# Moving ten rows of an adaLN modulation pair from VectorE to GpSimd in a two-layer trunk on one Trainium2 core

## What is computed

```python
cond = jax.nn.silu(c)                                  # 2048
for l in range(DEPTH):
    mod = (cond @ w_ada[l] + b_ada[l])[:, None, :]     # 2048 x 12288 per layer
    sh1, sc1, g1, sh2, sc2, g2 = jnp.split(mod, 6, axis=-1)
    u = x * (1.0 + sc1) + sh1
    y = mixer(u)
    x = layer_norm(ALPHA * x + (1.0 + g1) * y, ln_g[l, 0], ln_b[l, 0])
    u = x * (1.0 + sc2) + sh2
    y = conv_ffn(u, w_up[l], conv_w[l], conv_b[l], w_down[l])
    x = layer_norm(ALPHA * x + (1.0 + g2) * y, ln_g[l, 1], ln_b[l, 1])
```

## Time and profile before

| | us |
|---|---|
| median of 3 runs | 2282.24 (2281.42 to 2286.51) |
| the profiled execution | 2279.88 |
| its span, first to last instruction | 2278.1 |
| TensorE busy in it | 2234.2 |
| VectorE busy | 1695.1 |
| ScalarE busy | 1009.2 |
| GpSimd busy | 8.3 |
| mean granted TensorE clock | 0.993 of full speed |

### The profile page before, as it was taken

One profiled execution on the slowest core, in us unless ns is written; L12 is line 12 of the kernel. 1 busy time (PEld: TensorE's weight loads), 2 busy tenths in 40 slices (PEclk: granted clock), 3 DMA queues, 4 the chain that ended last, 5 costly groups with the idle time before them and its releaser, 6 DMA issues. The chain is left out here.

```text
span 2278.1 us, 27917 instructions
## 1 busy us (share of the span) xinstructions
PE 2234.2 (98%) x11205; PEld 1855.7 (81%) x11205; DVE 1695.1 (74%) x1671; ACT 1009.2 (44%) x1011; POOL 8.3 (0%) x19
## 2 busy tenths in 40 slices
PE   7999999999999999999999999999999999999999
PEld 3777777888887888888788888878888888888886
DVE  2889999768878878788877767684688756565565
ACT  2445344454433444443355444434544334444432
POOL 1000000000000000000000000000000000000000
PEclk9999999999999999999999999999999999999999
DMA  9999899868889978889787777865688756565653
GB/s 375 388 409 350 296 329 349 283 214 277 286 282 342 309 271 290 268 278 330 289 311 255 278 255 251 305 212 167 204 279 283 264 189 204 192 193 186 223 190 105
DMA packets 392227, 612.66 MB, mean 269 GB/s; under 512 B 21113, under 2 KB 205073, under 8 KB 390562
## 3 DMA queue, kind: packets, MB, share of 16 engines
q1 hardware_dynamic: 387314, 608.29, 76.4%
q10 hardware_dynamic: 4336, 2.33, 0.3%
q0 software_dynamic: 448, 0.25, 0.0%
HBM read 608.70 MB, written 2.10 MB: 268 GB/s over the span
## 5 line engine op out<-in xcount | busy, mean ns | idle before, releaser
L939 DVE TENSOR_TENSOR w_lo<-w_raw,w_hi 128x2048 fp32r<-128x2048 f32 x380 | 847.7, 2233 | 387.3 <-ACT w_hi L598 336.2
L598 ACT ACTIVATE w_hi<-w_raw 128x2048 fp32r<-128x2048 f32 x380 | 710.2, 1870 | 831.1 <-PE banks L1443 496.9
L1575 PE MATMUL banks<-u_hl,w_hi 128*128 128x512 f32 x2368 | 575.6, 392 | 3.3 <-ACT hid_tok L638 1.8
L1575 PEld LDWEIGHTS banks<-u_hl,w_hi 128*128 128x128 f32 x2368 | 432.9, 188 | 90.4 <-ACT hid_tok L638 2.7
L1443 PE MATMUL banks<-w_hi,u_hl 128*128 128x512 f32 x1920 | 478.7, 402 | 10.8 <-ACT u_hl L663 3.8
L1443 PEld LDWEIGHTS banks<-w_hi,u_hl 128*128 128x128 f32 x1920 | 362.5, 192 | 95.3 <-issue 16.3
L1583 PEld LDWEIGHTS banks<-u_hl,w_lo 128*128 128x128 f32 x2368 | 308.4, 191 | 15.6 <-DVE w_lo L939 1.2
L1583 PE MATMUL banks<-u_hl,w_lo 128*128 128x256 f32 x2368 | 313.3, 283 | 0.3 <-DVE w_lo L939 0.3
L1443 PE MATMUL banks<-w_hi,hid_hi 128*128 128x512 f32 x688 | 270.1, 393 | 0.0
L1443 PE MATMUL banks<-w_hi,hid_lo 128*128 128x512 f32 x688 | 267.8, 389 | 0.0
L955 DVE SCALAR_TENSOR_TENSOR ada_acc<-ada_w,silu_c,ada_acc 128x1024 f32<-128x1024 f32 x187 | 239.3, 1280 | 17.7 <-DMA ada_w<-in_w_ada 11.6
(11 more groups left out here) (229 smaller groups left out, 1247.8 us busy)
## 6 DMA issues: line engine op xcount, KB each, us to landing
ada_w<-in_w_ada SPq DMA_DIRECT2D x352, 512.0 KB, 6.7
w_raw<-in_w_up SPq DMA_DIRECT2D x344, 512.0 KB, 4.7
w_raw<-in_w_down SPq DMA_DIRECT2D x152, 512.0 KB, 4.9
w_raw<-in_w_qkv SPq DMA_DIRECT2D x96, 512.0 KB, 4.7
w_raw<-in_w_in_ab SPq DMA_DIRECT2D x64, 512.0 KB, 9.2
ada_w_more<-in_w_ada SPq DMA_DIRECT2D x32, 512.0 KB, 10.8
w_raw<-in_w_out_ab SPq DMA_DIRECT2D x32, 512.0 KB, 6.3
w_raw<-in_w_o SPq DMA_DIRECT2D x32, 512.0 KB, 5.1
```

The costliest lines, as they stand in the source:

```text
L598: nc.scalar.activation(whi[:, u % HL_SLOTS, 0:width], raw[:, u % RAW_SLOTS, 0:width], ACT.Copy).then_inc(w_hi, 1)
L939: nc.vector.tensor_tensor(wlo[:, u % HL_SLOTS, 0:width], raw[:, u % RAW_SLOTS, 0:width], whi[:, u % HL_SLOTS, 0:width].bitcast(f32), ALU.s ...
L1575: ins = nc.tensor.matmul(bank[banks[s] + i][:, :], tile(whi, k, s, i), uhl[:, kt].rearrange("p a s -> p (a s)"), start=first and k == 0, s ...
```

## The change

GpSimd takes rows 0 to 9 of pair 8. For each it waits until the row has landed, multiplies it in place in its slot by its column of silu(c) (for row 0, into the accumulator), waits for that product, and adds it to the accumulator. The semaphore `a_on_pool` counts the rows that it has taken; SP waits for it before it loads another row into such a slot. The loads of these ten rows stand with units 40 to 44, two each; before, nine stood with units 40 to 45 and row 9 with unit 52. VectorE takes the last six rows, two in each of units 52 to 54, and waits for all ten of GpSimd's ahead of the first. `STEP_NO` numbers the rows without GpSimd's for the waits on `a_step`.

```diff
+POOL_PAIR, POOL_ROWS = 8, 10
...
-    put([(8, r) for r in range(9)], first - 8, [2, 1, 2, 1, 2, 1])
+    for n in range(POOL_ROWS):
+        loads.setdefault(first - 8 + n // 2, []).append((POOL_PAIR, n))
     loads[first - 2] = [(9, r) for r in range(PE_ROWS[9])]
     put([(9, r) for r in range(PE_ROWS[9], 7)], first, [3], 1)
     put([(9, r) for r in range(7, KT)], first + 1, [3, 3, 3])
-    put([(8, r) for r in range(9, KT)], first + 4, [3, 2, 2])
+    put([(8, r) for r in range(POOL_ROWS, KT)], first + 4, [2, 2, 2])
...
+    steps = sorted((row for row in order if row[0] != POOL_PAIR or row[1] >= POOL_ROWS), key=order.get)
+    steps = {row: i for i, row in enumerate(steps)}
...
                     of, k = ROW_OF[old]
-                    if k < PE_ROWS.get(of, 0):
+                    if of == POOL_PAIR and k < POOL_ROWS:
+                        sp.wait_ge(a_on_pool, k + 1)
+                    elif k < PE_ROWS.get(of, 0):
                         sp.wait_ge(a_on_pe, PE_BASE[of] + k + 1)
                     else:
-                        sp.wait_ge(a_step, A0 + old + 1)
+                        sp.wait_ge(a_step, A0 + STEP_NO[of, k] + 1)
...
-                    dve.wait_ge(a_step, A0 + ROW_NO[m, r - 1] + 1)
+                    if (m, r) == (POOL_PAIR, POOL_ROWS):
+                        dve.wait_ge(a_on_pool, POOL_ROWS)
+                    else:
+                        dve.wait_ge(a_step, A0 + STEP_NO[m, r - 1] + 1)
...
+            acc = acc_of(POOL_PAIR)
+            pool.wait_ge(sem("silu_c"), 1)
+            pool.wait_ge(a_sum, SUM_NO[6, 0] + 1)
+            for r in range(POOL_ROWS):
+                slot, loads = ada_slot(POOL_PAIR, r)
+                w = ada_row_at(slot)
+                to = w if r else acc[:, :]
+                pool.wait_ge(a_loaded[slot], 16 * loads)
+                ins = nc.gpsimd.tensor_scalar(to, w, silu_c[:, r:r + 1], None, ALU.mult)
+                if r:
+                    ins.then_inc(sem("pool_product"), 1)
+                    pool.wait_ge(sem("pool_product"), r)
+                    pool.wait_ge(a_on_pool, r)
+                    ins = nc.gpsimd.tensor_tensor(acc[:, :], w, acc[:, :], ALU.add)
+                ins.then_inc(a_on_pool, 1)
```

More of the change, by code:

```diff
@@ L204, in ada_plan @@
     assert taken == sorted(taken)
-    return at, loads, order, sums, number, folds
+    steps = sorted((row for row in order if row[0] != POOL_PAIR or row[1] >= POOL_ROWS), key=order.get)
+    steps = {row: i for i, row in enumerate(steps)}
+    return at, loads, order, steps, sums, number, folds
 def build(nc, A, out):
@@ L344, in build @@
         a_on_pe = sem("ada_on_pe")
+        a_on_pool = sem("ada_on_pool")
         a_sum = sem("ada_summed")
@@ L398, in build @@
               (1, "down_b"): 20}
-        ADA_ROWS, ADA_LOADS, ROW_NO, ADA_SUMS, SUM_NO, ADA_FOLDS = ada_plan()
+        ADA_ROWS, ADA_LOADS, ROW_NO, STEP_NO, ADA_SUMS, SUM_NO, ADA_FOLDS = ada_plan()
         ROW_OF = {i: row for row, i in ROW_NO.items()}
@@ L1497, in ada_sum @@
                     warm(WARM_SUMS[m])
-                pe.wait_ge(a_step, A0 + ROW_NO[m, KT - 1] + 1)
+                pe.wait_ge(a_step, A0 + STEP_NO[m, KT - 1] + 1)
                 pe.wait_ge(a_out, SUM_NO[m, k] + 1)
@@ L1647, in up_first @@
                         if not layer:
-                            pe.wait_ge(a_step, A0 + ROW_NO[9, PE_ROWS[9]] + 1)
+                            pe.wait_ge(a_step, A0 + STEP_NO[9, PE_ROWS[9]] + 1)
                     unit(u, [(k, 4 * j + k) for k in range(4)], (uhi, ulo), j == 0, j == 3,
```

## The result

| | before | after |
|---|---|---|
| median | 2283.47 (4 runs, 2281.42 to 2286.51) | 2308.97 (4 runs, 2306.07 to 2311.73) |
| the profiled execution | 2279.88 | 2309.84 |
| its span | 2278.1 | 2307.7 |
| mean granted clock | 0.993 | 0.987 |

The change makes the kernel slower by 25.5 us; the ratio of the times is 1.0116, with a 95% interval of 1.0104 to 1.0128. Forecast were 10 us more, in a range that ended at 2306. The sign and the place were right, the size was not.

A forecast was written before the change was run, and what follows sets the result against it. TensorE, 98% busy, was taken as the bound, time changing only at its waits and slow clock. Late norm +8.2, slow clock +3.4, vanished wait -1.6: +10.0, forecast 2292 us, range 2278 to 2306.

The forecast's parts named there:

- turn-taking: Rival, 22%: GpSimd advances only while VectorE runs nothing with two SBUF inputs; norm's transposes +19.4, in all some +18, about 2300.
- Where it would happen: Ahead of the MLP's norm: GpSimd's last row delays load (9, 3), its matmuls, warm-up and the transposes, +8.2 us.
- Break-even, 3.6 us a row: Row 9 done at 344.9 + 8p against the slot's old freeing at 373.7; each 0.1 us above delays the norm 0.8.
- One product and one row fit ahead of row 2: GpSimd's start: rows 0 and 1 are finished before row 2 lands at 344.9, so eight rows follow from there.
- I take the upper end, p = 4.7: GpSimd's time per row, from its memset's 0.95 per stream times five streams; row 9 then done at 382.5.
- ten more: Within the turn-taking rival: p = 4.7 in place of the middle 3.35 adds ten us to its some +18.
- The landing, 6.5 us: Ahead of the norm: row (9, 3), issued at 382.6 once GpSimd frees the slot, lands at 389.1.
- The slow clock: At the norm: TensorE, waiting long, probably falls to its lower clock, at the price seen at pair 9's sum, +3.4 us.
- The wait of 1.6 goes: At pair 9's sum: its last rows gain time behind a late norm, so TensorE's wait vanishes, -1.6 us.
- The removal on VectorE, at nothing: Before 373.7 us: taking nine row instructions off VectorE gains nothing, since TensorE's own work hides them.
- The 1.1 us on VectorE's chain: Ahead of the norm: VectorE's tail starts 1.1 us earlier; only 0.58 usable unless pair 9's rows come earlier too.
- The rival without change: Rival, 25%: p between 3.2 and 3.9, row 9 done between 370.5 and 376.1, time 2281.6 to 2284.

## Why the prediction was right in sign and wrong in size

Two terms failed: p, the time of a GpSimd row (4.7 taken, 5.36 measured alone), and turn-taking, which was a rival and not a term (10.1 us). By the prediction's own sum p = 5.36 alone would give +15.2 and 2297.4, inside the range; it is the turns that carry the time beyond 2306. Point by point, in the time of before:

- **Where it would happen: right.** GpSimd's last row, the load of (9, 3), its matmuls, the warm-up and the transposes end last, in that order, and TensorE's waits name the DMA.
- **Break-even, 3.6 us a row: right.** Products alone end at 374.0 and cost nothing; with six, eight and ten rows GpSimd ends 8.1, 15.4 and 26.2 past the point, and the norm's transposes are 6.2, 13.3 and 24.2 late.
- **"One product and one row fit ahead of row 2": wrong**, by 3.4. They last until 348.3, not 344.9 (351.93 - 3.6). GpSimd starts at 338.6 and needs 3.0 + 5.36 for them alone, already 347.0.
- **"I take the upper end, p = 4.7": this step failed.** A row alone takes 5.36. The bound was made by scaling the memset (0.95) by streams, which gave the product two streams and 1.9 us; it takes 2.84. The memset is an instruction of GpSimd with no arithmetic and no operand to read, and was no upper bound for one that has both. From 338.6 on, 3.0 + 9 x 5.36 = 51.2 puts the last row at 389.8, **+16.1** over 373.7.
- **Turn-taking as a rival, not a term: this failed as well.** It adds **10.1** to that (399.9 against 389.8). I had laid 22 us of VectorE's work on top of the middle p. Both ends of that sum were off, p too low and the turns too many, and +18 was still short. The "ten more" that it gives for p = 4.7, some +28, was the nearest to what happened, by an overcount of the turns. My evidence against it, the memset beside a split, was none, since it reads nothing.
- **The landing, 6.5 us: too long.** With the queues empty (share 0.28) row (9, 3) landed 3.9 us after its issue, **-2.6**.
- **The slow clock: right that it falls, its price too high here.** The granted clock is 0.50, but TensorE has almost nothing to do in it: the last row's matmuls and the warm-up take 3.2 instead of 1.9, **+1.3**; no full unit is hit (unit 48's first part takes 3.91). Of 16.1 + 10.1 - 2.6 + 1.3 the 0.6 of waiting that TensorE had before is to be taken off: 24.3, with 24.2 in the trace for the transposes and 25.5 in the medians.
- **"The wait of 1.6 goes": wrong.** It is 2.07. Pair 9's later rows stood in the same queue behind GpSimd, so they came as much later as the norm.
- **The removal on VectorE, at nothing: right,** and for a stronger reason than I gave: with nobody taking the rows the kernel gains nothing that can be measured. The 1.1 us on VectorE's chain went the other way: the prediction named that the weights of the next units are queued behind SP's wait, and put no price on it. ScalarE waited 6.44 for them and the split ahead of the norm started at 374.5 instead of 373.7; with the longer split and addition the norm's scaling starts 4.9 later than before.
- **The rival without change** rested on p under 3.9; a row takes 5.36 alone. The Trainium skill's word of one-input work at roughly line-rate (GPSIMD Engine Reference, section 4.1) stood on its side: the prediction's estimate from it, 1024 elements at 1.2 GHz, is 0.85 for the product, which takes 2.84 here, so the measurement decides against it. The Trainium skill's figure for the add (the same page, section 3.1) holds nearly: half of 4497 ns is an estimate of 2.25, and the sum takes 2.34 here.

No version of the idea tried here beats the kernel before. Of those that do all the work the nearest is the one with ScalarE's products, 2.7 us over; the two that are even with the kernel before leave work out.

## What to carry to other kernels

Before work is moved from a busy engine to an idle one, ask what the kernel would gain if that work vanished. Here it was nothing, at most 2.3 us, so every cost on the other side was a loss. GpSimd's price for an instruction is to be measured alone and beside what runs next to it, as VectorE's instructions lengthen it and are lengthened by it, small one-input ones included. And a slot that a slow engine frees late holds up the whole load queue behind it, the weights of other engines among them (ScalarE waited 6.44 us here).

## What was not expected of the hardware

- GpSimd's f32 product by a column (one input) takes 2.84 us for 128x1024, longer than its sum of two tensors, 2.34; VectorE's takes 0.75. At 512 columns it is 1.56 against 1.26.
- A VectorE scaling of 128x512 with one SBUF input (0.41 alone) took up to 2.55 beside GpSimd's row, 0.80 in the mean; the norm's ten, six of 128x512 and four of 128x256, took 13.26 instead of 4.12 in the kernel. One with an input in PSUM was not touched.
- Turns are not shared evenly: a product and a split beside each other took 5.06 and 2.71 (2.84 and 2.28 alone), a sum and a split 4.27 and 4.42 (2.34 and 2.28 alone).
